# A table of 1152 bytes moves ahead of the weight panels, and everything between the two places lies 1152 bytes further on

## What is computed

```
block 1, twice:  proj = rmsnorm(h) @ w_in            # 1024 -> 6560
                 three attentions (latent, stick-breaking, differential), 272 tokens
                 h += (gated sum of out @ w_branch) @ w_out
                 h += relu(rmsnorm(h) @ w_ff1)**2 @ w_ff2          # 4096 wide
block 2, twice:  h += swiglu(modulated rmsnorm(h))   # 2816 wide, 512 tokens
                 h += retention (layer 0) or neighbourhood attention (layer 1)
                 h += swiglu(modulated rmsnorm(h))
```

## The kernel before, in words

| tile | start | modulo 256 | modulo 2048 |
|---|---|---|---|
| h | 16512 | 128 | 128 |
| xhi, xlo | 32896, 49280 | 128 | 128 |
| raw = wlo, whi | 65664, 82048 | 128 | 128 |
| modraw, sq, tmp, rs | 98432, 106624, 110720, 114816 | 128 | 128 |
| con, par, modv | 116864, 128672, 130048 | 128, 160, 0 | 128, 1696, 1024 |
| arena0 (f, g, r, n, o, m, all attention tiles) | 131200 | 128 | 128 |

## Time and profile before

### The profile page before, as it was taken

How to read it: one execution, slowest core, us unless ns; L and a number is a source line. 1 busy time by engine, 2 the same in 40 slices (tenths; PEclk the granted TensorE clock), 3 DMA queues, 4 the chain that set the end, 5 groups by cost and what they waited for, 6 DMA issues and landing times.

```text
span 3230.1 us, 48616 instructions
## 1 busy us (share of the span) xinstructions
PE 3136.0 (97%) x18046; PEld 2660.2 (82%) x18046; DVE 1724.8 (53%) x2409; ACT 1270.9 (39%) x2132; POOL 1950.4 (60%) x1285
## 2 busy tenths in 40 slices
PE   7999899999999999999999999999999999999998
PEld 6677899976779998888887777888888888886898
DVE  5665776655668865443435465544435443436554
ACT  4445555343555643222232443322223222235443
POOL 6658477514994975677567658678875777603000
PEclk9999999999999999999999999999999999999999
DMA  5323455632335663333443223334433443332354
GB/s 195 111 92 105 138 189 194 204 105 95 112 117 168 215 210 121 122 126 122 134 130 117 85 85 108 119 129 130 136 125 110 133 138 125 123 119 76 131 182 156
DMA packets 120280, 430.35 MB, mean 133 GB/s; under 512 B 13857, under 2 KB 17185, under 8 KB 119729
## 3 DMA queue, kind: packets, MB, share of 16 engines
q1 hardware_dynamic: 93632, 335.24, 31.7%
q0 software_dynamic: 24576, 86.46, 8.4%
q10 hardware_dynamic: 1904, 6.36, 0.5%
HBM read 426.95 MB, written 8.85 MB: 135 GB/s over the span
## 4 chain that ended last, share of the span: by engine, by line
PE 86%; POOL 5%; DVE 3%; ACT 2%; DMA 2%; issue 2%; ACTq 0%; DVEq 0%; SPq 0%; POOLq 0%
PE ps L484 22%; PE ps L486 21%; PE ps L485 21%; PE ps L511 2%; PE ps L581 2%; PE ps L582 2%; PE ps L583 2%; POOL macc L402 2%; DMA raw<-in_panels 2%; POOL modraw L400 2%; POOL mprod L400 1%; PE ps L525 1%; PE ps L530 1%; PE ps L526 1%; PE ps L986 1%
## 5 line engine op out<-in xcount | busy, mean ns | idle before, releaser
L1642 DVE TENSOR_TENSOR wlo<-raw,whi 128x1024 fp32r<-128x1024 f32 x632 | 856.0, 1355 | 914.6 <-ACT whi L1078 889.5
L1078 ACT ACTIVATE whi<-raw 128x1024 fp32r<-128x1024 f32 x632 | 668.4, 1058 | 1417.2 <-PE ps L486 901.2
L484 PE MATMUL ps<-xhi,whi 128*128 128x512 f32 (+2 forms) x2792 | 949.3, 340 | 3.1 <-DVE wlo L1642 2.5
L486 PE MATMUL ps<-xhi,wlo 128*128 128x512 f32 (+2 forms) x2792 | 934.6, 335 | 0.0
L485 PE MATMUL ps<-xlo,whi 128*128 128x512 f32 (+2 forms) x2792 | 933.7, 334 | 0.0
L484 PEld LDWEIGHTS ps<-xhi,whi 128*128 128x128 f32 x2792 | 531.8, 190 | 70.8 <-issue 14.8
L485 PEld LDWEIGHTS ps<-xlo,whi 128*128 128x128 f32 x2792 | 531.8, 190 | 51.8 <-issue 1.9
L486 PEld LDWEIGHTS ps<-xhi,wlo 128*128 128x128 f32 x2792 | 531.4, 190 | 50.2
L400 POOL TENSOR_SCALAR modraw<-modraw,cs 128x512 f32<-128x512 f32 x288 | 552.1, 1917 | 27.6
L400 POOL TENSOR_SCALAR macc<-modraw,cs 128x512 f32<-128x512 f32 x36 | 70.5, 1958 | 745.2 <-PE ps L511 602.5
L400 POOL TENSOR_SCALAR mprod<-modraw,cs 128x512 f32<-128x512 f32 x252 | 445.8, 1769 | 19.0 <-POOL macc L402 0.2
(11 more groups left out here) (362 smaller groups left out, 4752.9 us busy)
## 6 DMA issues: line engine op xcount, KB each, us to landing
raw<-in_panels SPq DMA_DIRECT2D x632, 512.0 KB, 3.3
modraw<-in_mod POOLq DMA_DIRECT2D x144, 512.0 KB, 4.4
bias_by_column<-in_rpb POOLq DMA_DIRECT2D x16, 476.2 KB, 8.3
bia<-bias_by_column POOLq DMA_DIRECT2D x32, 96.0 KB, 2.6
rtab<-in_rtab ACTq DMA_DIRECT2D x2, 1312.0 KB, 7.4
wuq<-in_wuq ACTq DMA_DIRECT2D x2, 768.0 KB, 6.7
con<-in_con SPq DMA_DIRECT2D x1, 1345.5 KB, 13.7
h<-in_x SPq DMA_DIRECT2D x1, 1088.0 KB, 6.7
```

Of the source, the lines that this page charges most:

```text
L484: pe.matmul(out, w_hi, x_hi, start=start, stop=False)
L486: return pe.matmul(out, w_lo, x_hi, start=False, stop=stop)
L1078: act.activation(whi[:, s * PW:(s + 1) * PW], raw[:, s * PW:(s + 1) * PW], ACT.Copy).then_inc(hi_split, 1)
L1642: dve.tensor_tensor(wlo[:, s * PW:(s + 1) * PW], raw[:, s * PW:(s + 1) * PW], whi[:, s * PW:(s + 1) * PW].bitcast(F32), ALU.subtract).then ...
```

## The change

The declaration of `modv`, the modulation vector (2 x 72 x 2 floats, 1152 bytes in each partition), moves up, ahead of `raw`:

```
         xhi, xlo = sb("xhi", NC * T2, F32R), sb("xlo", NC * T2, F32R)
+        modv = sb("modv", DEPTH * MODT * 2)
         raw_at = place[0]
         raw = sb("raw", RAW * PW)
         wlo = nc.alloc_sbuf_tensor_at("wlo", [P, RAW * PW], F32R, offset=raw_at)
         whi = sb("whi", RAW * PW, F32R)
...
         con = sb("con", C_N)
         par = sb("par", P_N)
-        modv = sb("modv", DEPTH * MODT * 2)
         arena0 = place[0]
```

## The result

The changed kernel takes **3274.36 us** (median; 3272.1 to 3279.54), against 3239.43 for the kernel before, measured beside it: ratio 1.0111, 95% interval 1.0092 to 1.0129. It is slower by 34.9 us. The forecast was 3238 with 3212 to 3274 as the whole range; rival A had 3266 to 3274, and the measured time lies just above both.

What follows compares the result with a forecast made beforehand. The prediction took the distances between TensorE's matmul starts to bound the kernel. Its three terms, 0 + 0 + 0 on the 3230.1 us span, plus the 8.4 us by which the runs' median exceeded it, gave 3238 us, range 3212 to 3274.

Steps and rivals of the forecast that it cites:

- rival A: Block 2's 512-column matmuls: distance 128 doesn't settle, reads get in each other's way; 28 to 36 us slower; chance 0.30.
- What bounds the kernel: Whole kernel: matmuls cover 97% of the span, so any change acts through the distances between matmul starts.
- part (1): Distance of weights from activations: 8640 block 2 matmuls go from 0 to 128 modulo 256; taken as 0 us.
- The last reading: Block 2, all at distance 0, after a pause: nine steps of 231.1 ns before settling at 227.
- the third: Block 1's token tiles, 512 columns: distance 128 looked 4 to 5 ns dearer.
- the second: Block 1, 272 columns over all four distances: surcharge 13.0 ns, against 13.3 to 13.8 at distance 0.
- chunk 2: Block 1's token tiles at distance 128: four steps of 232.5 ns, 5.4 ns dearer, pricing the slower case at 36 us.
- block 1 keeps its time: Block 1: shifting by 128 leaves the same four distances as often as before, so 0 us.
- Parts (2) and (3): Other moved tiles (0, bounds -3 and +3 us) and panels landing at 0 modulo 256 (0, about 1 us either way).
- Rival B: Distance 0 is the worst of four: -1.3 ns on all 8640 block 2 matmuls, -11 us, 3227 us; chance 0.25.
- Rival C: Block 2: at distance 128 the reads no longer meet, the surcharge goes; 118 us at most, to 3120; chance 0.08.
- Rival D: Weights' place alone or another period counts, so block 1's 126.3 ns moves too; chance shared among the others.

Runs made afterwards that it cites:

- the sweep: Kernel before with weights moved to distances 32, 64, 96, 160, 192 and 224 modulo 256 from all activations, one kernel each; ratios 1.0042 to 1.0149.
- e19: Kernel before with block 1's feed-forward input and hidden layer in rows of 320 floats, all at distance 0 from the weights; 3236.05 us, ratio 0.9995.
- e3: Kernel before with every tile 128 bytes further on, so all places change and no distance does; 3239.38 us, ratio 1.0004.
- e2: Kernel before with modv between whi and modraw, so modraw, sq, tmp, rs, con and par move and the panels don't; 3239.38 us, ratio 0.9998.
- e1: Kernel before with 128 bytes left free ahead of raw and 128 after par, modv staying after par; 3277.45 us, ratio 1.013.
- e4: Kernel before with only xhi and xlo moved to distance 128 from the weights, g, r and n staying at 0; 3266.11 us, ratio 1.0094.
- e10: Kernel before with 192 bytes free ahead of raw and 64 after par, weights at distance 192 from all activations; 3253.86 us, ratio 1.0042.
- e16: Kernel before with distance 64 in block 1's feed-forward and in block 2's last layer, the 256-column one; 3226.95 us, ratio 0.9966.
- e18: Kernel before with xlo alone 128 bytes further on modulo 256; 3254.93 us, ratio 1.0047.
- e9: Kernel before with 64 bytes free ahead of raw and 192 after par, weights at distance 64 from all activations; 3267.2 us, ratio 1.0092.

## Why the prediction was wrong, point by point

**What bounds the kernel: right.** The time went through the distances between starts: 35.5 us by steps, 34.9 measured.

**The step that failed** is in part (1): "The last reading takes the ground from the third, and the second is the nearest to a plain comparison over many matmuls: I take 0 for all 8640." Measured, it is +5.7 and +6.2 ns on the 6672 with 512 columns and -1.3 on the 1968 with 256. Two mistakes are in that sentence. The third reading, chunk 2 of the earlier trace rows, was the only one with 512 columns at distance 128. I let it be explained away by the earlier trace rows, nine steps after a pause at distance 0. These show that something else can also give 231 ns; they don't show that distance 128 doesn't. That chunk 2 agrees with the settled 232.5 ns to a tenth is luck, though: it is four unsettled steps read from rounded times, and to the nanosecond they average 234.0. The same trace had more to say. Over all token tiles of 128 tokens in block 1, pauses and stretches at the lower clock left out, the steps of a chunk average 230.1 ns at distance 0 (26 steps), 231.0 at 64 (38), 233.1 at 128 (26) and 233.4 at 192 (40). That is the order that the sweep found for settled token tiles (226.84, 228.97, 233.00, 233.32), at half the size. It gives a direction and not a price: in the changed kernel, where the same chunks take other distances, the means are 230.8, 230.1, 231.5 and 233.5 ns for 0, 64, 128 and 192, and 128 is dearer than 0 by 0.7 only. And I carried 272 columns over to 512, by the thought that the surcharge hardly depends on the columns. At distance 0 that nearly holds (13.8 and 13.3 ns; 12.0 with 272 columns in e19); over the distances it doesn't. At 64 the surcharge is 20.0 ns with 512 columns and 7.2 with 256.

**"If only the distance modulo 256 counts, block 1 keeps its time": right.** 126.3 ns in both; e3 shows that it isn't the place, and the sweep that the period is 256.

**Parts (2) and (3), nothing each: right** in the time, shown by e2 and e3.

**Rival A had the place and the price.** By chunk 2 alone it gave 5.4 x 6672 = 36 us; the 512-column steps took 38.1 us. The price by chunk 2 owes its closeness to the luck named above. And its condition was misnamed: the surcharge does settle, in a fixed cycle. **Rival B** was right about the 256 columns (-1.3 ns each), and worth 2.6 us, since it holds there alone: of the four distances in block 1, 0 is the dearest at 256 columns (119.96 ns) and the cheapest at 512. **Rival C** is refuted at every distance tried: the lowest at 512 columns is 226.85. At 256 columns half of the surcharge does go, but at distance 64 and not at 128. **Rival D** is refuted by e3 (the place alone) and by x and g in the sweep (another period); block 1 agrees, but a period of 512 would have left it alone too.

**The rules weighed.** The sentence "PE and ACT never wait on anyone" of the Trainium skill (SBUF — State Buffer, section Who interferes with whom) and its two independent read ports would have made the change do nothing. e1 and e4 disagree: with the same instructions, the place of the load against the stream moves a step from 226.9 to 232.7 ns. I had seen that the rule doesn't explain and should have given that more weight. The 215.8 ns that the Trainium skill gives for lone matmuls (TensorE: Matmul & The Clock Gate, section Back-to-back issue gap) were reached at none of eight distances; all steps here have a weight load each.

## What to carry to other kernels

Where a kernel is a long row of matmuls with a weight load for each, look at the place of the loaded operand against the streamed one, modulo 256 bytes. In this kernel, with float32r operands, it is worth up to 1.5% of the time between the best and the worst of eight distances, with no instruction changed. Find the best for each number of columns by trying it; 0 was best for 512 and 64 for 256, and a best for one size is a poor one for the other. And when a trace passes through the disputed condition even briefly, gather every such passage and compare the means before you explain one reading away. Unsettled passages like these give a direction, not a price. A reading of another condition that comes out alike (231.1 ns after a pause) doesn't contradict them.

## What the runs showed of the hardware that was not expected

- At full granted clock a run of load-and-stream steps settles into a pattern that repeats after a few steps (one before; two, seven or, with 256 columns, five in the changed kernel; three in e10: 226, 229, 232) and depends on the two operands' distance modulo 256 bytes: means of 226.85 to 234.28 ns with 512 columns, 113.92 to 119.97 with 256.
- Stream minus load is what counts: turning the roles turns the sign (228.96 and 228.97 ns at 192 and 64).
- One arrangement can have several settled costs: 113.9 and 117.4 ns (e16), 231.4 and 233.6 (e18), changing across a mod group; 118.7 and 120.0 (e4, x at 256 columns).
- With 256 columns, the surcharge over the columns' 106.7 ns is 6.6 ns at distance 64 (the 527 steps of e9) where it is 13.3 at distance 0.
- VectorE is busy for less time in every kernel whose 512-column steps are dearer: 1694.7 to 1718.5 us, against 1724.1 to 1730.5 in those that keep distance 0 there.
